# Expert stage of a two-layer trunk: 256-column expert tiles of one slot group, and block transposes in place of TensorE transposes

## The reference

```python
logits = (xn @ w_router).astype(jnp.float32)
top_vals, top_idx = lax.top_k(logits, TOP_K)
top_w = jax.nn.softmax(top_vals, axis=-1)
...
for e in range(N_EXPERTS):
    out = out + combine[..., e:e + 1] * swiglu(xn, w_gate[e], w_up[e], w_down[e])
# swiglu(x, g, u, d) = (silu(x @ g) * (x @ u)) @ d;  g, u: 1024 x 3584, d: 3584 x 1024
```

## Time and profile before

| | us |
|---|---|
| three runs | 1725.45, 1729.42, 1731.07 |
| median | 1729.42 |
| span of the profiled execution | 1727.6 |
| start of the first expert product in the trace | 755.5 |
| TensorE busy, share of the span | 96% |
| VectorE, ScalarE, GpSimd busy | 32%, 24%, 15% |

### The profile page before, as it was taken

The page is one execution under the profiler, slowest core; times in us unless marked ns, Lnnn a source line. Parts: engine busy times, 40 slices in busy tenths (PEclk is TensorE's granted clock), DMA queues, the critical chain, the costliest instruction groups (busy, mean ns, idle before and its releaser), DMA issues.

```text
span 1727.6 us, 32135 instructions
## 1 busy us (share of the span) xinstructions
PE 1655.4 (96%) x14514; PEld 1004.5 (58%) x14514; DVE 552.4 (32%) x836; ACT 410.2 (24%) x524; POOL 252.5 (15%) x338
## 2 busy tenths in 40 slices
PE   7889989999989999899999999999999999999996
PEld 6868989999989879853332333433333323334333
DVE  6557567444454675431010011110010100111102
ACT  5442344444454523310010010100010100101002
POOL 3877278000000461000000000000000000000000
PEclk9989999999999999989999999999999999999998
DMA  9702574555545324569989999989999989999980
GB/s 279 247 25 74 153 225 148 195 179 187 179 139 172 122 74 149 218 270 358 399 324 362 397 362 383 360 341 388 391 357 398 349 336 400 358 384 377 351 332 25
DMA packets 192649, 465.12 MB, mean 269 GB/s; under 512 B 9600, under 2 KB 91520, under 8 KB 192512
## 3 DMA queue, kind: packets, MB, share of 16 engines
q1 hardware_dynamic: 189600, 461.40, 72.3%
q0 software_dynamic: 416, 1.05, 0.3%
q10 hardware_dynamic: 2496, 0.61, 0.2%
HBM read 461.98 MB, written 1.05 MB: 268 GB/s over the span
## 4 chain that ended last, share of the span: by engine, by line
PE 88%; POOL 4%; DVE 4%; ACT 2%; issue 1%; ACTq 0%; DVEq 0%; POOLq 0%
PE work L627 28%; PE acc L892 23%; PE acc L920 17%; PE ssm_y L892 11%; PE acc L627 5%; PE work L903 1%; PE ssm_y L737 1%; PE work L728 1%; DVE arena L1532 1%; PE work L641 1%; POOL arena L1700 1%; DVE arena L1263 1%; PE acc L698 0%; DVE parts L1245 0%; POOL arena L1703 0%
## 5 line engine op out<-in xcount | busy, mean ns | idle before, releaser
L627 PE MATMUL work<-xs,parts 128*128 128x256 f32 x3648 | 463.4, 287 | 16.8 <-DVE xs L1252 13.6
L627 PEld LDWEIGHTS work<-xs,parts 128*128 128x128 f32 x3648 | 450.1, 194 | 28.1 <-issue 25.0
L892 PE MATMUL acc<-ring,arena 128*32 128x512 f32 (+1 forms) x4096 | 435.2, 543 | 0.7 <-issue 0.7
L920 PE MATMUL acc<-ring,arena 128*32 128x512 f32 x2688 | 294.4, 592 | 1.4 <-ACT arena L1176 1.4
L1245 DVE TENSOR_TENSOR parts<-ring,parts 128x2048 fp32r<-128x2048 f32 x94 | 222.8, 2375 | 177.6 <-ACT parts L1010 177.5
L892 PEld LDWEIGHTS acc<-ring,arena 128*32 128x32 f32 x4096 | 131.0, 110 | 247.8 <-issue 227.2
L892 PE MATMUL ssm_y<-ring,arena 128*32 128x512 f32 (+1 forms) x2048 | 239.3, 539 | 0.0
L1010 ACT ACTIVATE parts<-ring 128x2048 fp32r<-128x2048 f32 x94 | 179.1, 1910 | 122.6 <-PE work L627 69.5
L920 PEld LDWEIGHTS acc<-ring,arena 128*32 128x32 f32 x2688 | 85.8, 110 | 196.6 <-issue 192.9
L1541 DVE TENSOR_TENSOR arena<-arena,acc 64x256 f32<-64x256 f32 (+1 forms) x32 | 12.5, 390 | 561.2 <-ACT arena L1171 561.2
L1171 ACT ACTIVATE arena<-acc 64x512 f32<-64x512 f32 (+1 forms) x96 | 51.6, 538 | 556.6 <-PE ssm_y L892 555.0
(11 more groups left out here) (244 smaller groups left out, 1098.2 us busy)
## 6 DMA issues: line engine op xcount, KB each, us to landing
ring<-in_moe_w_gate SPq DMA_DIRECT2D x112, 1024.0 KB, 7.2
ring<-in_moe_w_up SPq DMA_DIRECT2D x112, 1024.0 KB, 9.4
ring<-in_moe_w_down SPq DMA_DIRECT2D x112, 1024.0 KB, 8.7
ring<-in_w_in SPq DMA_DIRECT2D x44, 1024.0 KB, 6.7
ring<-in_dense_w_gate SPq DMA_DIRECT2D x14, 1024.0 KB, 5.0
ring<-in_dense_w_up SPq DMA_DIRECT2D x14, 1024.0 KB, 5.0
ring<-in_dense_w_down SPq DMA_DIRECT2D x14, 1024.0 KB, 4.9
ring<-in_w_out SPq DMA_DIRECT2D x8, 1024.0 KB, 12.0
```

What stands on the lines that cost most here:

```text
L627: last = nc.tensor.matmul(out_ap, a, b, start=start and n == 0, stop=stop and n == len(pairs) - 1, skip_group_check=shared)
L892: last = nc.tensor.matmul(region(x, ns), xe[:, k, c:c + GRP], w[:, kk, half * ns:half * ns + ns], start=k == 0, stop=k == KT - 1)
L920: last = nc.tensor.matmul(acc[GRP * q:GRP * q + GRP, b, :], eh[:, kt % tiles, c:c + GRP], w[:, kk, half * OUT_COLS:half * OUT_COLS + OUT_C ...
```

## The change

Each set's product now streams 256 weight columns per matmul in all four sets. In the three wide sets the four strips of the array hold the same slot group, and each strip streams another quarter (`CHUNK` = 256 columns) of the gate weights, then of the up weights: twice as many matmuls of half the length. The result is laid out with chunks on the partitions (32 slots of each), gates of the three slot groups side by side in `gu_low` and two thirds of the up part in `gu_high`. Silu becomes one activation of 128 partitions and 768 columns, the product two VectorE instructions. A VectorE block transpose (`STREAM_TRANSPOSE`, 128 by 768) writes `eh` directly; `turn`, its PSUM groups and both copies are gone. `eh` is double buffered. The down weights are loaded so that each partition takes two neighbouring rows of 4 KB, in line with the order in which the block transpose leaves the hidden columns, and one unit load at the edge between gate/up and down units waits for a pair later than before. `gate_up` itself waits for `erow_ready`. `combine_rows` is split: three groups after set 0's product, the fourth after set 1's, followed by the turn of the slot weights. Every gather uses four quarters of the model width.

```diff
-    SETS = [(0, 512), (1024, 512), (2048, 512), (3072, 256)]
+    SETS = [(0, 1024), (1024, 1024), (2048, 1024), (3072, 512)]
...
                 for j in range(MR, IU):
-                    if j % 2 == 0:
+                    if j == FIRST_DOWN - 1:
+                        sp.wait_ge(pair_used, i * PAIRS + ((j + 1 - MR) // 2 + 1))
+                    elif j % 2 == 0 and j != FIRST_DOWN:
                         sp.wait_ge(pair_used, i * PAIRS + ((j - MR) // 2 + 1))
                     load_unit(j, e)
...
             def gate_up(which, i, first_slot):
-                ns, pairs = SETS[which][1], GU_PAIRS[which]
+                chunks, pairs = SETS[which][1] // CHUNK, GU_PAIRS[which]
+                if not isinstance(i, int) or i or which:
+                    pe.wait_ge(erow_ready, i * NSET + which)
...
-                        for x in range(4 * NG):
-                            half, g = x % (2 * NG) // NG, x % NG
-                            w = gate if x < 2 * NG else up
-                            c = first_slot + g * GRP
-                            last = nc.tensor.matmul(region(x, ns), xe[:, k, c:c + GRP],
-                                                    w[:, kk, half * ns:half * ns + ns], start=k == 0,
-                                                    stop=k == KT - 1)
+                        for kind in range(2 if chunks == 4 else 1):
+                            for g in range(NG):
+                                begins = k == 0 and (g in (0, 2) if kind == 0 else g == 1)
+                                x = xe[:, k, first_slot + g * GRP:first_slot + g * GRP + GRP]
+                                for q in range(4):
+                                    if chunks == 4:
+                                        w, c = (gate, up)[kind], q
+                                    else:
+                                        w, c = (gate, up)[q // 2], q % 2
+                                    out_ap = gate_region(g, q) if kind == 0 else up_region(g, q)
+                                    last = nc.tensor.matmul(out_ap, x, w[:, kk, c * CHUNK:(c + 1) * CHUNK],
+                                                            start=begins, stop=k == KT - 1,
+                                                            skip_group_check=True)
...
                 gate_up(0, i, first_slot)
                 if not isinstance(i, int) or i:
-                    combine_rows(i)
-                turn(0, i)
+                    combine_rows(i, range(WB))
+                gate_up(1, i, first_slot)
+                if not isinstance(i, int) or i:
+                    combine_rows(i, range(WB, 2 * TT))
                 bank = begin(Group(("tw", 0), i), i)
...
-                gate_up(1, i, first_slot)
-                for which in range(1, NSET):
-                    down(which - 1, i)
-                    turn(which, i)
-                    if which < NSET - 1:
-                        gate_up(which + 1, i, first_slot)
+                for which in range(2, NSET):
+                    down(which - 2, i)
+                    gate_up(which, i, first_slot)
+                down(NSET - 2, i)
...
             def silu_gates(which, i):
...
+                if SETS[which][1] == 4 * CHUNK:
+                    nc.scalar.activation(esilu[:, :], gu_low[:, 0:EW], ACT.Silu).then_inc(silu_set, 1)
...
+            def hidden_turn(which, i):
                 tiles = SETS[which][1] // P
+                dve.wait_ge(erow_ready, i * NSET + (which + 1))
+                nc.vector.transpose(eh[:, which % 2, 0:tiles, :].rearrange("p f (g n) -> p f g n", g=NG),
+                                    erow[:, 0:tiles * SLOTS].rearrange("p (g i f) -> p f g i", g=NG, f=tiles))\
+                    .then_inc(eh_ready, 1)
```

More of the change, by code:

```diff
@@ L84, in trunk_kernel @@
         else:
-            EXPERT += [("D", which, n ^ 1) for n in range(D_UNITS[which])]
+            EXPERT += [("D", which, n) for n in range(D_UNITS[which])]
         PAIRS_AT[step] = len(EXPERT) // 2
     IU = len(EXPERT)
+    FIRST_DOWN = EXPERT.index(("D", 0, 0))
     PAIRS = IU // 2
@@ L175, in trunk_kernel @@
         GROUPS += [("item", i, g) for g in ITEM_GROUPS if g[0] != "gather" and (i or g[0] != "comb")]
-        GROUPS += [("item", i, ("gather", q)) for q in range(gathers(i))]
+        GROUPS += [("item", i, ("gather", q)) for q in range(QUARTERS if gathers(i) else 0)]
     ITEM0 = len(GROUPS)
@@ L467, in moe_view @@
             kind, which, n = EXPERT[j]
-            width = D if kind == "D" else 2 * SETS[which][1]
+            width = D if kind == "D" else SETS[which][1]
             return moe_slot(j % MR).rearrange("p (k n) -> p k n", n=width)
@@ L847, in _, with gather_half @@
                 .then_inc(work_done, 1)
-            def gather_one(half, item):
-                bank = begin(Group(("gather0", half)) if item is None else Group(("gather", half), item), item)
+            def gather_half(half):
+                bank = begin(Group(("gather0", half)))
                 for q in range(HALF):
@@ L869, in _ @@
             for half in range(2):
-                gather_one(half, None)
+                gather_half(half)
             def unit(j, i):
@@ L959, in _ @@
                     pe.wait_ge(pick_ready, i // 2 + 2)
-                for q in range(gathers(i)):
-                    if gathers(i) == 4:
-                        gather_two(Group(("gather", q), i), q)
-                    else:
-                        gather_one(q, i)
+                for q in range(QUARTERS if gathers(i) else 0):
+                    gather_quarter(q, i, gathers(i) * SLOTS)
                 down(NSET - 1, i)
@@ L1195, in _ @@
                     silu_gates(which, i)
-                    hidden_act(which, i)
-                if gathers(i) == 4:
-                    move_pair([Group(("gather", q), i) for q in range(2)])
-                elif gathers(i):
-                    move_one(Group(("gather", 0), i))
+                if gathers(i):
+                    for q in range(QUARTERS // 2):
+                        move_quarter(q, i, gathers(i) * SLOTS)
                 rows_high(i)
@@ L1206, in _ @@
                     silu_gates(which, i)
-                    hidden_act(which, i)
-                move_one(Group(("gather", 0), i))
+                for q in range(QUARTERS // 2):
+                    move_quarter(q, i, SLOTS)
                 rows_high(i)
@@ L1593, in _ @@
                 expert(i)
-                if gathers(i) == 4:
-                    move_pair([Group(("gather", 2 + q), i) for q in range(2)])
-                elif gathers(i):
-                    move_one(Group(("gather", 1), i))
+                if gathers(i):
+                    for q in range(QUARTERS // 2, QUARTERS):
+                        move_quarter(q, i, gathers(i) * SLOTS)
                 rows_low(i)
```

184 lines of the change are left out of this document (84 added, 100 removed).

## The result

The changed kernel takes 1693.14 us (median of four runs, 1692.77 to 1693.36) against 1730.14 for the kernel before beside it. The ratio is 0.9788, with a 95% interval of 0.9776 to 0.9799. The prediction was 1694.5.

What follows compares the result with a forecast made beforehand. TensorE was taken as the bound, with DMA close behind. Savings 14.1 + 1.8 + 3.3 + 18.9 - 3.4 = 34.7 us took the span from 1727.6 to 1692.9, median 1694.7; stated prediction 1694.5, range 1687 to 1710.

Steps and rivals of the forecast that it cites:

- Turns 1 and 2: TensorE's six transposes between a down product and product 2 or 3: 16 turns by 0.88 us, 14.1 us saved.
- Turn 3: After down 2: 0.36 us saved in five items that gather (1.8 us), 1.09 in items 1, 3, 5 (3.3 us).
- The boundary: Between set 0's and set 1's products: shortened to 2.35 us, with 0.95 us behind set 1's product; 18.9 us saved in total.
- The clock: At boundaries 1, 3, 5 it holds, worth 4.5 us; rival: it falls at all eight, 1706.7 us, chance 0.07.
- The narrower matmul: In the wide products, 256-column instructions cost 0.14 us more per product, +3.4 us over 24 sets.
- VectorE's transpose: Block transpose of 768 columns after each wide set: about 1.0 us, bounds 423 ns and 2.1 us, none on the path.
- DMA: Rival in the expert stage: the weight stream sustains under some 375 GB/s, about 10 us lost, 1705 us; chance 0.05.
- The narrow stream: Rival in all 24 wide products: 256-column stream slower than set 3 shows; 10% slower gives 1744 us; chance 0.09.
- Edits at nothing: Down weights' layout, later load wait, four-quarter gathers, added VectorE instructions, startup and tail: no time gained or lost.

Runs made afterwards that it cites:

- delayed silu: The changed kernel with one idle 512-column activation ahead of silu in the three wide sets: 1697.78 us, ratio 0.9817.
- staged start: The changed kernel with set 1's product starting its first 16 gate matmuls once silu is done, before VectorE's product: 1688.78 us, ratio 0.9766.

## Why the prediction was right, point by point

**Turns 1 and 2: right.** 0.88 us by 16 was 14.1; the rows after give (811.71 - 800.49) - (810.01 - 799.69) = 0.90, 14.4, and putting idle transposes back cost 15.9 in time.

**Turn 3: right.** 0.36 in five items and 1.09 in three were predicted. The gather now starts 10.42 us after down 2's start instead of 10.80, 0.38; items 1, 3 and 5 run down 2 and down 3 in one piece, 984.24 - 968.79 = 15.45 against 993.22 - 976.62 = 16.60, 1.15.

**The boundary: right, with the chain a little short of my value.** 2.35 us was predicted and 2.17 (item 0) and 2.23 (item 1) came: silu took the 0.81 that the step from 256 to 512 columns gave, the second VectorE product began 0.34 us after the first and not 0.42, and from VectorE's end to TensorE's start it was 0.06 us, not 0.15. Item 3, at 2.58, was longer than predicted. The delayed silu and the staged start both show that this chain is what TensorE waits for. Behind product 1 1.01 us against 0.95. Item 0 saved 1.06, items 2, 4 and 6 1.99 each and item 7 2.07, items 1, 3 and 5 3.49, 3.12 and 3.34, the falls of the clock included.

**The clock: the result was right, the reason is not shown.** I expected it to hold at items 1, 3 and 5 because the boundary has fewer waits, and it held. The term was 4.5 of the 34.7 us; the falls cost 4.3 in the trace of before. From item 1 on every kernel of the new order has one wait at this boundary or none: 0.46 us in the changed kernel, 1.07 with the combine in one piece, 0.95 with the delayed silu, 0.46 with six transposes behind it. None of them lost the clock. Of the kernels of the old order, the one with the split alone has two waits (0.73 and 0.76 us) and lost it at two items; the kernel before and the one with the narrow matmul have three (0.73, 0.46 and 0.16) and lost it at three and five. So the length of one wait and the transposes by themselves are out, and several short waits stay possible: no run puts them into the changed kernel. They are not sufficient either, since items 2, 4, 6 and 7 of the kernel before have them and no fall. The Trainium skill, TensorE: Matmul & The Clock Gate, section A second HAM failure mode, has TensorE idling for short times between groups of matmuls, in a bf16 kernel that cycles through PSUM banks, as what makes the clock swing. The falls in the kernel before fit it; the five kernels here with one idle time at the same place and no fall show that one such time was not enough. The cause of the falls stays open.

**The narrower matmul: right, slightly too dear.** 0.14 a product was read from set 3, 0.11 came: 2.6 us instead of 3.4.

**VectorE's transpose: priced too low, and of no effect.** I took 1.0 us by width with 2.1 as the bound above; it takes 1.60 for 768 columns and 0.92 for 384. The transpose hides under the next product, as argued. The estimate of 1.9 us from the Trainium skill, VectorE: DVE Perf Modes, section The three transpose paths, was nearer, though its figure is for bf16. The rule of the Trainium skill, VectorE: DVE Perf Modes, section Rules for kernel authors, that sends such a transpose to TensorE would have kept 14 us on the path.

**The rivals.** The clock did not fall. DMA did not take over, and the margin was larger than I had it on both sides. The stream sustains 409 GB/s, not 385. And the 118 us from which I took an item's length are those of the short items; the mean item went from 119.4 to 114.9 us, a demand of 383 GB/s and not 388. The narrow stream was no slower than set 3 showed.

**Edits at nothing: nearly right.** The gather takes 867.22 - 861.81 = 5.41 us where it took 5.31, 0.1 in each of five items, and the tail behind the last down product is 0.3 us shorter in this trace.

**The sum.** By the rows: 14.4 for turns 1 and 2, 1.9 and 3.5 for turn 3, 1.1 + 8.0 + 10.0 at the boundary, less 2.6, is 36.3 us; the spans differ by 36.3. The prediction had 34.7. Each of the five terms was a little on the low side of the gain, the narrower matmul most (0.8), so the small miss is no sum of large errors that cancel.

## What to carry to other kernels

A transpose that TensorE does between its products costs its own time there, however cheap it looks; moved to an idle engine it may take nearly twice as long (1.60 us here against 0.90) and still be free, provided that a product of another set lies between it and its reader. A wait that such a move adds is worth pricing as a chain, instruction by instruction, and then asking which matmuls touch only what the first link of the chain has released. A busy share of the DMA engines near one does not show whether they could move another 6%, as they could here: take work from the other engine and read the rate. And a price per matmul has to count the instructions that one matmul is made of.

## What the runs showed of the hardware

- The weight stream sustains 409 GB/s at a DMA share of 1.02, while a stretch of the kernel before had the same share at 385 GB/s.
- Four column strips that stream four different pieces of the weights run as fast as four that stream two: 20.73 and 20.74 us.
- A VectorE block transpose of float32, SBUF to SBUF, takes 1.60 us for 128 by 768 and 0.92 us for 128 by 384. Of six transposes in a row between two products, TensorE's path shows 0.90 us.
- The granted clock fell to the lower level at three, five and two of the eight boundaries in the traces of the three kernels with the old order. It fell at none in the six kernels with the new one that do all the work, whose idle times there are between 0 and 2.46 us. One execution of each is traced (two of the changed and of the staged kernel), and the mean clock of whole executions of one kernel varies: 0.977 to 0.981 before.
- In the kernel that leaves out half the products, and so waits for weights all the time, the clock reads 0.93 to 0.94 of full on average.
